# Final projection of a two-block program: slabs, residual and operand parts placed ahead of the recurrence's last chunk, and slab 0 split between the first scalings

## The reference, cut to what matters

```python
def second_block(x, c, norm_g, w_ada, b_ada, w_in, ...):
    c_act = jax.nn.silu(c)
    for l in range(DEPTH):
        mod = c_act @ w_ada[l] + b_ada[l]
        shift, scale, gate = jnp.split(mod, 3, axis=-1)
        h = rms_norm(x, norm_g[l]) * (1.0 + scale[:, None, :]) + shift[:, None, :]
        proj = h @ w_in[l]
        ps = token_shift(proj[..., :D_SHIFT], mu_shift[l])
        pa = proj[..., D_SHIFT:]
        y_r, g_r = rwkv7_mix(ps, ...)          # the recurrence: 16 chunks of 64 rows, one after the other
        q, ka, va, g_a = jnp.split(pa, 4, axis=-1)
        y_a = chunk_band_attention(q, ka, va, ...)   # no row depends on another's output
        y = jnp.concatenate([y_r * jax.nn.silu(g_r), y_a * jax.nn.silu(g_a)], axis=-1)
        x = x + gate[:, None, :] * (y @ w_out[l])
    return x
```

## Time and profile before

| | us |
|---|---|
| runs (3) | 2535.12, 2537.77, 2538.06 |
| median | 2537.77 |
| the profiled execution | 2540.11 |
| its span in the trace | 2538.3 |
| PE busy | 2403.1 (95%) |
| DVE busy | 1405.2 (55%) |
| ACT busy | 930.0 (37%) |

### The profile page before, as it was taken

The page is one execution under the profiler, slowest core; times in us unless marked ns, Lnnn a source line. Parts: engine busy times, 40 slices in busy tenths (PEclk is TensorE's granted clock), DMA queues, the critical chain, the costliest instruction groups (busy, mean ns, idle before and its releaser), DMA issues. The chain is left out here.

```text
span 2538.3 us, 41309 instructions
## 1 busy us (share of the span) xinstructions
PE 2403.1 (95%) x17918; PEld 1960.7 (77%) x17918; DVE 1405.2 (55%) x2453; ACT 930.0 (37%) x1547; POOL 78.4 (3%) x61
## 2 busy tenths in 40 slices
PE   6999977999999999999999999899999998899879
PEld 5777766788888888888888888677788776677767
DVE  4575766565445555543555554555455557666753
ACT  3445432444333333422333423353233242333341
POOL 0000000000000000000000000011000002100000
PEclk9999988999999999999999999899999998898999
DMA  6443310544113333333333333333222213101034
GB/s 196 125 143 109 91 35 8 167 128 121 50 51 91 93 98 100 91 96 96 100 99 93 96 108 112 113 97 118 78 80 80 60 43 121 37 7 41 2 120 146
DMA packets 358188, 230.94 MB, mean 91 GB/s; under 512 B 9460, under 2 KB 332148, under 8 KB 357880
## 3 DMA queue, kind: packets, MB, share of 16 engines
q1 hardware_dynamic: 355272, 222.74, 29.3%
q10 hardware_dynamic: 2736, 5.57, 0.6%
HBM read 210.45 MB, written 17.83 MB: 90 GB/s over the span
## 5 line engine op out<-in xcount | busy, mean ns | idle before, releaser
L1354 PE MATMUL PS<-SR 128*128 128x512 f32 (+1 forms) x2400 | 957.6, 399 | 41.8 <-DVE SR L1880 38.1
L1356 PE MATMUL PS<-SR 128*128 128x512 f32 (+1 forms) x2400 | 933.9, 389 | 0.0
L1355 PE MATMUL PS<-SR 128*128 128x512 f32 (+1 forms) x2400 | 933.7, 389 | 0.0
L1880 DVE TENSOR_TENSOR SR<-SB,SR 128x1024 fp32r<-128x1024 f32 (+1 forms) x328 | 396.3, 1210 | 393.1 <-ACT SR L2587 392.5
L1354 PEld LDWEIGHTS PS<-SR 128*128 128x128 f32 x2400 | 452.5, 189 | 152.2 <-DVE SR L1880 39.6
L1356 PEld LDWEIGHTS PS<-SR 128*128 128x128 f32 x2400 | 452.4, 189 | 95.5
L1355 PEld LDWEIGHTS PS<-SR 128*128 128x128 f32 x2400 | 453.4, 189 | 88.6 <-issue 1.9
L2587 ACT ACTIVATE SR<-SB 128x1024 fp32r<-128x1024 f32 (+1 forms) x328 | 338.9, 1035 | 270.9 <-DMA SB<-in_w_down 102.6
L1749 PEld LDWEIGHTS PS<-SB 64*64 64x64 f32 x4096 | 130.4, 138 | 34.8 <-issue 22.9
L1749 PE MATMUL PS<-SB 64*64 64x64 f32 x4096 | 143.4, 224 | 7.8 <-DVE SB L2467 6.6
L1340 PE MATMUL PS<-SB 128*128 128x128 f32 (+2 forms) x688 | 107.5, 293 | 27.2 <-DVE SB L2345 10.0
(11 more groups left out here) (269 smaller groups left out, 2486.2 us busy)
## 6 DMA issues: line engine op xcount, KB each, us to landing
SB<-in_w_in SPq DMA_DIRECT2D x110, 512.0 KB, 3.9
SB<-in_w_up SPq DMA_DIRECT2D x88, 512.0 KB, 3.8
SB<-in_w_out SPq DMA_DIRECT2D x32, 512.0 KB, 4.5
SB<-in_w_down SPq DMA_DIRECT2D x32, 512.0 KB, 4.2
SB<-in_w_ada SPq DMA_DIRECT2D x12, 1024.0 KB, 6.4
asides<-SB SPq DMA_DIRECT2D x36, 256.0 KB, 2.6
SB<-in_wkv SPq DMA_DIRECT2D x16, 512.0 KB, 4.0
SB<-in_wq SPq DMA_DIRECT2D x16, 512.0 KB, 4.3
```

The lines of the kernel that those rows point to most:

```text
L1354: pe.matmul(out, whi[:, k - k0, :], hi[k], start=(k == 0), stop=False)
L1355: pe.matmul(out, whi[:, k - k0, :], lo[k], start=False, stop=False)
L1356: i = pe.matmul(out, wlo[:, k - k0, :], hi[k], start=False, stop=(k == j.K - 1))
L1880: v.tensor_tensor(m.f32r(a, kn * cn), m.f32(a, kn * cn), m.f32r(a + 1024, kn * cn).bitcast(F32), SUB).then_inc(*on("split.v", p))
```

## The change

1. At the start `cols` goes alone ahead on ACT's queue, `cst` after `raw(1)` and `rows` after `raw(7)`. Slab 0 is split after `raw(4)`. The three `rms_add` steps come together after `raw(7)`.
2. At the end a mark "near" is set after `pre` of pair 7 and the output of pair 6. From it on the first two slabs of `fin0` are fetched (slots 0 and 1), four of the eight residual tiles of half 0 come back, and all eight parts of half 0 are made; the low parts lie in place, over the inputs they are made from. Parts 4 to 7 have marks of their own (x0 to x3).
3. `fin0` begins after the state of pair 7. Tiles 0 and 1 may run before "most"; slabs 326 and later, the other four residual tiles and the parts of half 1 wait for it. `slab` splits none ahead at slab 325.

```diff
@@ second
-        self.OP2 = [self.parts(W0 + 8192, W0 + 12288)[0:2],
-                    ([self.f32r(a + 512 * i, 512) for a in (W0 + 24576, G0) for i in range(4)],
-                     [self.f32r(a, 512) for i in range(8) for a in [X0 + 512 * i if i < 4 else W0 + 1024 * i - 3584]])]
+        self.OP2 = []
+        for h, (a, b) in enumerate(((W0 + 24576, W0 + 8192), (W0 + 12288, G0))):
+            low = [((X0 if h else W0 + 16384) + 512 * i if i < 4 else W0 + 1024 * (i - 4) + 512 * h) for i in range(8)]
+            self.OP2.append(([self.f32r(x + 512 * i, 512) for x in (a, b) for i in range(4)], [self.f32r(x, 512) for x in low]))
@@ ends
-        yield from self.after(("seq", 7), *[("band", j, n) for j in range(4) for n in range(4)])
+        yield from self.after(("pre", 7), ("seq", 6))
+        yield [("mark", "near"), ("fetch", self.wall, 2), ("back", 0, 0, "near")]
+        for k in range(4):
+            yield [("fin_part", 0, k, "near")]
+        for j in range(4):
+            yield from self.after(*[("band", j, n) for n in range(4)])
+            yield [("mark", f"x{j}"), ("fin_part", 0, 4 + j, f"x{j}")]
+        yield from self.after(("state", 7))
         self.banks = self.eight
-        yield [("mark", "most"), ("fetch", self.wall), ("back", 0)]
+
+    def residual(self):
+        yield from self.after(("seq", 7))
+        yield [("mark", "most"), ("back", 0, 4, "most")]
         self.done.add("most")
-        for k in range(8):
-            yield [("fin_part", 0, k, "most")]
@@ compose
         for k in range(8):
-            self.emit(("raw", k), *[("rms_add", "mix0", i) for i in {5: [0], 7: [1, 2]}.get(k, [])])
+            self.emit(("raw", k), *{1: [("load_c", "cst")], 4: [("split", 0, 1)], 7: [("load_c", "rows")]}.get(k, []))
+        self.emit(*[("rms_add", "mix0", i) for i in range(3)])
...
-                        self.ends(), T("fin0"), self.after("parts1"), T("fin1")),
+                        self.ends(), T("fin0", 0, 2), self.after("most"), T("fin0", 2, 6), self.after("parts1"), T("fin1")),
...
-                  *[self.lane(units) for _ in range(3)], self.ended())
+                  *[self.lane(units) for _ in range(3)], self.residual(), self.ended())
@@ vector and scalar program
-    def slab(q):
-        limit = min(q + 3, o.wall) if q < o.wall else min(q + 2, len(o.slabs))
+    def slab(q, ahead=3):
+        limit = min(q + ahead, o.wall) if q < o.wall else min(q + (1 if q == o.wall + 1 else 2), len(o.slabs))
@@ sync program
             if p >= o.wall:
-                ended("most")
+                ended("near" if p < o.wall + 2 else "most")
```

More of the change, by code:

```diff
@@ L329, in second @@
         self.src2 = [self.rr[h] + [self.yaT[:, j, hs(h)] for j in range(4)] for h in range(2)]
-        self.OP2 = [self.parts(W0 + 8192, W0 + 12288)[0:2],
-                    ([self.f32r(a + 512 * i, 512) for a in (W0 + 24576, G0) for i in range(4)],
-                     [self.f32r(a, 512) for i in range(8) for a in [X0 + 512 * i if i < 4 else W0 + 1024 * i - 3584]])]
-        self.back = [tiles(v3(f32(X0 + 2048, 2048), 4)) + tiles(v3(f32(X0 + 5632, 2048), 4)), tiles(v3(work(4096, 4096), 8))]
+        self.OP2 = []
+        for h, (a, b) in enumerate(((W0 + 24576, W0 + 8192), (W0 + 12288, G0))):
+            low = [((X0 if h else W0 + 16384) + 512 * i if i < 4 else W0 + 1024 * (i - 4) + 512 * h) for i in range(8)]
+            self.OP2.append(([self.f32r(x + 512 * i, 512) for x in (a, b) for i in range(4)], [self.f32r(x, 512) for x in low]))
+        self.back = [tiles(v3(work(10240, 2048), 4)) + tiles(v3(f32(X0 + 5632, 2048), 4)), tiles(v3(work(4096, 4096), 8))]
 class Job:
@@ L1276, in ended @@
         yield from self.after(*[("band", j, n) for j in range(4) for n in range(8)])
-        yield [("mark", "rec"), ("back", 1)]
+        yield [("mark", "rec"), ("back", 1, 0, "rec"), ("back", 1, 4, "rec")]
     def split_pairs(self):
@@ L1986, in ev_out @@
         w.wait_ge(*at("gemm.pe", q))
-        w.wait_ge(*at(f"back{j.half}", 7))
+        w.wait_ge(*at(f"back{j.half}{t // 4}", t // 4 * 4 + 3))
         w.wait_ge(*at("ada.v", "mod", 11))
@@ L2552, in fin_part @@
         v.tensor_tensor(lo[k], m.src2[h][k], hi[k].bitcast(F32), SUB).then_inc(*on("fin.v", "lo", h, k))
-    do = dict(mark=lambda name: S.mark("v", name), slab=slab, raw=raw, ev_scaled=ev_scaled, ev_gate=ev_gate, ev_add=ev_add, ev_swish=ev_swish,
+    do = dict(mark=lambda name: S.mark("v", name), slab=slab, split=slab, raw=raw, ev_scaled=ev_scaled, ev_gate=ev_gate, ev_add=ev_add, ev_swish=ev_swish,
               ev_conv_m=ev_conv_m, conv_o=conv_o, ev_conv_f=ev_conv_f, ev_up=ev_up, ev_shift=ev_shift, ev_out=ev_out, rms_add=rms_add,
@@ L2572, in scalar_program, with load, slab @@
     split = [0]
[L2574 to L2579, removed]
+    def load(name="cols"):
+        a.dma_start(m.fixed[name], m.d[name]).then_inc(*on(name, 0, by=16))
+    def slab(q, ahead=3):
+        limit = min(q + ahead, o.wall) if q < o.wall else min(q + (1 if q == o.wall + 1 else 2), len(o.slabs))
         while split[0] < limit:
@@ L2909, in fin_part @@
         a.activation(m.OP2[h][0][k], m.src2[h][k], ACT.Copy).then_inc(*on("fin.a", "hi", h, k))
-    do = dict(mark=lambda name: S.mark("a", name), load=load, slab=slab, raw=raw, ev_scaled=ev_scaled, ev_copy=ev_copy, ev_swish=ev_swish,
+    do = dict(mark=lambda name: S.mark("a", name), load=load, load_c=load, slab=slab, split=slab, raw=raw, ev_scaled=ev_scaled, ev_copy=ev_copy, ev_swish=ev_swish,
               ev_conv_m=ev_conv_m, conv_t=conv_t, ev_conv_f=ev_conv_f, ev_up=ev_up, ev_shift=ev_shift, ev_out=ev_out, rms_sq=rms_sq,
@@ L2981, in ended, with slab @@
                 w.wait_ge(*x)
-    def slab(q):
-        limit = min(q + 4, o.wall if q < o.wall else len(o.slabs))
+    def slab(q, ahead=4):
+        limit = min(q + ahead, o.wall if q < o.wall else len(o.slabs))
         while fetched[0] < limit:
@@ L3082, in band_load, with back @@
                 *on(f"bg{j % 2}", j, h, by=16))
[L3084 to L3087, removed]
+    def back(h, k0, mark):
+        ended(mark)
+        for k in range(k0, k0 + 4):
+            sp.dma_start(m.back[h][k], m.spilled[:, k, 512 * h:512 * h + 512]).then_inc(*on(f"back{h}{k0 // 4}", k, by=16))
     def end():
```

## The result

The changed kernel took **2552.29 us** (median of four runs, 2547.41 to 2553.46) against 2537.91 of the kernel before (2535.12 to 2539.89): ratio 1.0058, 95% interval 1.0040 to 1.0076. The profiled execution has a span of 2550.6 us, 12.3 more than before. The forecast was 2548.0 with a range of 2537 to 2554, and "slower" had 0.62: direction and range hold. The median rose by 14.4 us where 10.5 were forecast. In the profiles the start is worth -3.2 us up to the mark "near" and the end +15.5 us; the other 2 us of the median are inside what the interval leaves open (10.2 to 19.3 us). The parts of the sum don't all hold.

What follows compares the result with a forecast made beforehand. PE was taken as the bound, with 38.1 us of waits on DVE's low parts. Start -4.8, walk +8.3, tail +0.8 and clock +6.2 gave +10.5, thus 2548 us on the median; 8-in-10 range 2537 to 2554.

Steps and rivals of the forecast that it cites:

- slower: Whole run: clock and delays near the walk, 2543 to 2553 us; chance 0.62.
- the stall: PE's 8.2 us wait after the recurrence, before a low part; forecast to move behind two tiles, not go.
- The start: Kernel start: slab 0 lands and is split earlier, tile 1 begins at 24.8 instead of 29.59, minus 4.8 us.
- up to 1.8 given back: Between tiles 0 and 1: if tile 1's first matmuls run at half pace, up to 1.8 us of gain is lost.
- The first gap: Before the last pair's `seq_u`: PE idle about 7.0 us, with all eight parts in front of `seq_x`.
- The second and third gap: PE idle 5.0 us before tile 0 of `fin0` and 9.0 us before tile 2, behind splits.
- The stall closes: Rival at tile 1's last matmul: "most" comes early enough, the 8.2 us wait goes, 2522 us; chance 0.08.
- The walk at the full clock, +8.3: End of kernel, stepped to tile 2 at 2449.2 against 2440.95 for the same work before: plus 8.3 us.
- The tail, +0.8: Last unit's outputs come behind tile 7, leaving one wait for ACT's copy open: plus 0.8 us.
- `back` of half 1 is late for one `ev_out` only, with three banks free: Tail: claim that half 1's late `back` costs nothing.
- The clock, +6.2: End: half clock behind the gaps before `seq_u` (3.5) and tile 0 (2.7), plus 6.2 us; tile 2's cancels.
- The sum: Whole run: -4.8 + 8.3 + 0.8 + 6.2 = +10.5 us; the end alone plus 15.3.

Runs made afterwards that it cites:

- slot_reuse: Changed kernel with slabs 326 and 327 put in the slots tiles 0 and 1 just used, 326 split ahead of `band_s` (3, 4): 2537.1 us, ratio 1.0012.
- kept_clock_2: Changed kernel with unread transposes on PE: 66 ahead of `seq_u`, 42 ahead of tile 0, 72 ahead of tile 2: 2539.2 us, ratio 1.0019.
- evacuated_later: Changed kernel with the evacuation of fin1's first tile moved behind the next slab's split: 2545.3 us, ratio 1.0034.
- start_warm: Kernel before with only the change's start, plus 58 unread transposes in PE's one wait of 8.2 us: 2532.2 us, ratio 0.9976.
- parts_in_holes: Changed kernel with the eight parts under one mark, put one by one where DVE stood idle in the kernel before: 2540.8 us, ratio 1.0019.
- all_closed: parts_in_holes plus slot_reuse's slots, slab 324 split behind `seq_u` (7, 1), slab 326 behind `band_y` (2, 6): 2520.9 us, ratio 0.9939.
- one_mark: Changed kernel with one mark for parts 4 to 7 in place of four: 2546.5 us, ratio 1.0040.
- end_alone: Changed kernel with the start undone, so only the end of the change: 2552.3 us, ratio 1.0061 to the kernel before.
- kept_clock: Changed kernel with unread transposes on PE, 52 ahead of the last pair's `seq_u` and 34 ahead of `fin0`'s first tile: 2546.6 us, ratio 1.0042.

## Why the prediction was right, and where it wasn't

The mechanism came true: the start shorter, the eight parts in front of the recurrence, the stall moved behind two tiles and not closed, three falls of the clock instead of one. Several sizes did not, and they cancel.

- **The start, -4.8.** Right for the changed kernel's profile: the landing was at 13.2 for 13.1, the first matmul at 15.60 for 15.4, tile 1 at 24.87 for 24.8. Between there and "near" 1.5 us were lost again, 1.0 of it around one place (PE's timeline), where the granted clock was at 0.50 for longer than in the kernel before; 96 small matmuls took 3.86 us, 3.16 before:

```profile
2361.50 3.86 PE L1759 MATMUL PS<-SB 64*64 64x64 f32 x96
...
2360.60:2363.00 2.40, 2.37 (x33) 0.50 0.00 0
```

The bound "up to 1.8 given back" is a matter of the execution: it occurred in six of twelve profiles, not in the changed kernel's. In the sum it should have stood at half its size.
- **The first gap.** Right in kind, 7.6 for 7.0. The rounds are 1.39 for 1.4; ACT began 1.05 us behind the mark's last releaser, not 0.27, hence the 0.6.
- **The second and third gap.** Right, 5.07 for 5.0 and 8.9 for 9.0. The stall had moved behind two tiles; in slot_reuse, where slab 326 does not wait for the mark, it is gone. "The stall closes" was rightly kept out by PE's order.
- **The walk at the full clock, +8.3.** kept_clock_2 shows it without the clock: tile 2 at near + 60.9, where I had near + 59.55 (2449.2 - 2389.65). So +9.6, if the kernel before stands at near + 51.3 at this amount of work; that point is worked out (2440.95 - 2389.65) and was not measured.
- **The tail, +0.8.** Mis-sized. PE's wait for ACT's copy, forecast at 0.8, is 1.5 (L1697). And "`back` of half 1 is late for one `ev_out` only, with three banks free" is true and priced the wrong thing. That `ev_out` stands on DVE's queue in front of a split, and ACT's copy stands behind its output DMA: 2.0 us, 1.8 by evacuated_later. Without the clock the stretch behind tile 2 is 158.1 - 60.9 = 97.2, and in the kernel before, warmed, 145.9 - 51.3 = 94.6: +2.6, by the same worked-out point.
- **The clock, +6.2.** The mechanism was right: three falls for one. The size was too large. The sum of kept_clock_2 (6.1) and start_warm (2.7) leaves 3.4. By place, each term came out smaller: 2.8 to tile 0 for my 3.5, and 2.1 to tile 2 for my 2.7. The third did not cancel, as I had said: behind tile 2 the half clock costs 1.2 us, behind the kernel before's one stall 2.7. It ended 3 us behind tile 2's first matmul, and 6 us behind tile 0's in the kernel before (2.4 GHz back within 2452 to 2456, and within 2434 to 2436). In the other five profiles with the third gap it is 3.7 to 5.1 us, so this part depends on the execution. Also, "both gaps are longer than the one that let it fall" is wrong as it stands: 7.0 and 5.0 us are shorter than 8.2; they are longer than the 4 us of it that had passed when the clock fell.
- **The sum.** 9.6 + 2.6 + 3.4 = +15.6 for the end, forecast +15.3. That it meets the measured +15.5 is no check, since the three are differences of the same four stretches. Two terms were short by 3.1 and one was long by 2.8: that the total fits is luck.
- By the Trainium skill (TensorE: Matmul & The Clock Gate, section "HAM oscillation — how this bites in real kernels") the price is paid once per gap. The falls agree, one to each of the three long gaps in the changed kernel's profile; the price is not the same in each (2.8, 2.1 and 1.2 us, and 2.7 in the kernel before).

## What to carry to other kernels

Work that is brought forward goes in front of something: look on each in-order queue for what stands behind it, also behind the evacuation that waits for a moved transfer. Eight small operations made PE wait 7.6 us as a block in front of the recurrence, and not at all before the same `seq_u` when they stood in that engine's own holes (parts_in_holes). A wait that hangs on a mark moves with the mark; it closes only when its resource comes from another place, here the slots of the tiles just done. Each of these repairs alone left the kernel no faster than before (parts_in_holes 1.0019, slot_reuse 1.0012); with all waits closed it was 0.6% faster (all_closed, 0.9939).

## What was not expected of the hardware

- In the changed kernel and in one_mark the clock came back about 21 us behind "near", though the wait before it ended 2.3 us sooner in one_mark; with the wait of 7.6 us it came back at near + 22 in end_alone, slot_reuse and evacuated_later.
- Filling 6 of 7.6 us with matrix work did not keep the clock, filling all but 0.3 did. But filling all but 1.9 of 8.2 us kept it in start_warm, and all but 1.2 of 5.1 in kept_clock: what is left of the gap doesn't decide it alone.
- The clock also fell behind short waits: 1.83 us in parts_in_holes, 1.86 in slot_reuse.
- The same instructions with the same waits (1.40, 1.83) kept the clock in one execution and lost it in another; the mean granted clock of 2250 to 2350 us was between 0.90 and 0.97 without any edit there. What decides this stays open.
